# Page loads of odd samples issued by the ScalarE queue, those of even samples by the sync engine

## The reference

```
past_rows = pool[layer, page_table]            # 16 pages of 128 rows per sample, K and V, 2 heads of 128
s = q . k * HEAD_DIM ** -0.5 - slope * dist    # then a mask: the 16 best blocks of 64 rows
p = softmax(s)
o = p . v
```

## Time and profile before

| | |
|---|---|
| median of 3 runs | 3255.11 us (3253.07 to 3260.55) |
| the profiled execution's own time | 3257.21 us |
| its span, first to last instruction | 3255.5 us |
| busy: TensorE matmul, weight load | 2653.4 us (82%), 2007.5 us (62%) |
| busy: VectorE, ScalarE | 860.5 us (26%), 272.5 us (8%) |
| read from HBM, written | 669.20 MB, 17.50 MB |
| mean granted TensorE clock | 0.872 of full speed |
| the phase of the 10 turns | from 1722.9 us to 1934.5 us of the span |

### The profile page before, as it was taken

How to read it: one execution, slowest core, us unless ns; L and a number is a source line. 1 busy time by engine, 2 the same in 40 slices (tenths; PEclk the granted TensorE clock), 3 DMA queues, 4 the chain that set the end, 5 groups by cost and what they waited for, 6 DMA issues and landing times. The chain is left out here.

```text
span 3255.5 us, 46977 instructions
## 1 busy us (share of the span) xinstructions
PE 2653.4 (82%) x19541; PEld 2007.5 (62%) x19541; DVE 860.5 (26%) x2027; ACT 272.5 (8%) x598; POOL 21.1 (1%) x68
## 2 busy tenths in 40 slices
PE   5999995999982577783666459649999999999997
PEld 4767673777751576672644337546777676677764
DVE  0121212000038455415344320222111211211124
ACT  0010101000010000000112110100010010001001
POOL 0000000000000000000000000000000000000000
PEclk9999996999985688766557779859999999999998
DMA  6888854242210000001374763229999999999991
GB/s 238 318 321 316 321 193 162 103 155 103 103 39 13 15 2 2 2 1 29 109 230 105 182 186 123 84 76 405 409 392 402 396 398 392 403 394 392 399 398 44
DMA packets 180772, 679.98 MB, mean 209 GB/s; under 512 B 38188, under 2 KB 39038, under 8 KB 141918
## 3 DMA queue, kind: packets, MB, share of 16 engines
q1 hardware_dynamic: 177780, 673.92, 55.3%
q10 hardware_dynamic: 2884, 4.50, 0.4%
HBM read 669.20 MB, written 17.50 MB: 211 GB/s over the span
## 5 line engine op out<-in xcount | busy, mean ns | idle before, releaser
L571 PE MATMUL bank<-sb_hT,sb_w_in 128*128 128x296 f32 x1408 | 353.6, 415 | 3.9 <-PEq L462 3.9
L571 PEld LDWEIGHTS bank<-sb_hT,sb_w_in 128*128 128x128 f32 x1408 | 269.0, 191 | 88.5 <-issue 5.9
L2418 PE MATMUL bank<-sb_gate_w,sb_x_picked 128*64 128x256 f32 x2048 | 322.1, 379 | 0.7 <-DMA sb_up_w<-in_w_up_dram 0.7
L2418 PE MATMUL bank<-sb_up_w,sb_x_picked 128*64 128x256 f32 x2048 | 322.1, 379 | 0.0
L2443 PE MATMUL bank<-sb_down_w,sb_hiddenT 128*64 128x512 f32 x1024 | 226.8, 594 | 9.0 <-ACT sb_x_picked L2478 9.0
L397 PE MATMUL bank<-sb_cmp_xT,sb_cmp_w 128*128 128x254 f32 x1024 | 223.4, 379 | 6.7 <-ACT sb_cmp_xT L213 5.8
L397 PEld LDWEIGHTS bank<-sb_cmp_xT,sb_cmp_w 128*128 128x128 f32 x1024 | 193.2, 190 | 39.0 <-ACT sb_cmp_xT L213 8.4
L2418 PEld LDWEIGHTS bank<-sb_gate_w,sb_x_picked 128*64 128x64 f32 x2048 | 175.1, 137 | 59.9 <-issue 17.1
L2402 PE MATMUL bank<-sb_select,sb_h2rows 128*128 128x128 f32 x1632 | 188.9, 278 | 18.6 <-DVE sb_give L2512 18.6
L2418 PEld LDWEIGHTS bank<-sb_up_w,sb_x_picked 128*64 128x64 f32 x2048 | 175.3, 137 | 45.7
L2402 PEld LDWEIGHTS bank<-sb_select,sb_h2rows 128*128 128x128 f32 x1632 | 185.6, 194 | 24.9 <-DVE sb_give L2512 18.7
(11 more groups left out here) (535 smaller groups left out, 2823.9 us busy)
## 6 DMA issues: line engine op xcount, KB each, us to landing
sb_gate_w<-in_w_gate_dram SPq DMA_DIRECT2D x64, 2048.0 KB, 10.5
sb_up_w<-in_w_up_dram SPq DMA_DIRECT2D x64, 2048.0 KB, 15.0
sb_down_w<-in_w_down_dram SPq DMA_DIRECT2D x64, 2048.0 KB, 9.3
sb_w_ada<-in_w_ada_dram SPq DMA_DIRECT2D x48, 2048.0 KB, 10.9
sb_w_in<-in_w_in_dram SPq DMA_DIRECT2D x11, 4096.0 KB, 13.3
sb_cmp_raw<-in_cache_cmp_kv_dram SPq DMA_DIRECT2D x128, 256.0 KB, 7.6
sb_sample_kv<-in_cache_slc_kv_dram SPq DMA_DIRECT2D x128, 256.0 KB, 5.4
sb_w_out<-in_w_out_dram SPq DMA_DIRECT2D x4, 4096.0 KB, 13.9
```

The source lines that it names most:

```text
L571: ins = pe.matmul(k.bank[m][:, 0:NX], w[r][:, t, m * P:(m + 1) * P], k.hT[:, t, :], start=(t == 0), stop=(t == KT - 1))
L2418: ins = pe.matmul(bank[b][64 * half:64 * half + 64, col:col + 256], x[:, t, b * 64:b * 64 + 64], w[i][:, t % CK, half * 256:half * 256 + 256],
```

## The change

ScalarE issues the page units with odd m, that is those of odd samples, from unit 11 on, and the sync engine keeps the page units with even m and all windows. ScalarE does so at the end of a turn, behind `exp(n)` (in turn 3 behind `pre_exp` as well), for those of the units 4(n - 1) + 11 to 4n + 10 that are odd and no windows, after a wait for `s_av` >= n, which is the value that the sync engine waits for at these units. `load_pages` itself is the same, and so are the buffers, the semaphores that the loads raise and the units loaded ahead.

```diff
@@ the sync engine's block of phase_attend_samples
                 for m in range(N_UNITS, 4 * N_TURN):
                     if m == 12:
                         sp.wait_ge(s_pre, SCORED)
                         load_kc(k, sp, 1)
                     if m == 20:
                         sp.wait_ge(s_pav, 1)
                         load_vc(k, sp, 1)
+                    if m // 4 % (N_CH + 1) and m % 2:
+                        continue
                     sp.wait_ge(s_av, (m - N_UNITS) // 4 + 1)
                     (load_pages if m // 4 % (N_CH + 1) else load_window)(k, A, sp, m)
@@ the ScalarE block, in the loop over the turns n
                     exp(n)
                     if n == 3:
                         pre_exp(1)
+
+                    for m in range(max(N_UNITS, 4 * (n - 1) + N_UNITS), min(4 * n + N_UNITS, 4 * N_TURN)):
+                        if n and m // 4 % (N_CH + 1) and m % 2:
+                            act.wait_ge(s_av, n)
+                            load_pages(k, A, act, m)
```

## The result

The changed kernel takes **3290.56 us** in the median of 4 runs (3283.85 to 3296.36), against 3254.6 us (3253.07 to 3260.55) for the kernel before: ratio 1.0106, 95% interval 1.0082 to 1.0131. It is slower by 36 us where 26 were forecast. The median stands 0.56 us above the upper end of the range, which is less than the runs differ among themselves. The profiled execution has a span of 3291.4 us and took 3293.18.

What follows compares the result with a forecast made beforehand. TensorE's waits before turns 2 to 9 for each release's opening page unit were taken as the bound; sharing the DMA engines adds 26.6 us to 3257.21, 3283.8, less 2.1 for the median: 3281 us forecast, range 3253 to 3290.

Steps and rivals of the forecast that it cites:

- What bounds the phase: Before turns 2 to 9 TensorE waits for the unit opening each release; eight waits, 64.9 us together, on the path.
- A page's rate is set by its transfer, not its issue: Page loads: 1.17 us of DMA-engine transfer at 225 GB/s, slower than the 1.07 us issue.
- the rival: No change: two queues near 400 GB/s, opening unit lands as before, bound by issue and ScalarE's hold; 3256 us, chance 0.15.
- ScalarE's issue price of 1.07 us: Each of 52 loads added to ScalarE costs the sync engine's 1.07 us; bounds 0.32 and 1.97 us.
- the hold of 8.6 us: Issuing two units holds ScalarE 8.6 us before the next turn's key copies; hidden, at worst +11 us.
- The shared page time: Opening unit's pages interleave with the sync engine's: 3.16 + 7.5 x 1.17 = 11.9 us, against 7.84 at turn 2.
- the rule of slots: Opening unit lands 3.16 us plus a number of page times after the values; 7 to 8 when shared, 7.5 taken.
- Turn 4: Wait for unit 19, ScalarE's, beside three windows: 12.6 us against 7.84, +4.8; +7.4 if whole windows pass between pages.
- the lateness: At turn 4 ScalarE issues unit 19 some 2.2 us later than the sync engine did, behind its exponentials.
- Turns 5 and 6: Turn 5, window 23 beside ScalarE's unit 25: +3.0 us; turn 6, ScalarE 0.6 us late: 12.4 against 9.84, +2.6.
- 16 pages in a period of now 23 us, so the queues drain each time: Each turn's 16 pages take 18.7 us of transfer within a 23 us period, leaving no backlog for the next release.
- The rivals: No change, 3256 us, chance 0.15; faster, shared page time under 0.69 us (380 GB/s), 3247 us, chance 0.08.

Runs made afterwards that it cites:

- e10: Changed kernel plus a sync-engine wait: it starts its own units only when the pages of the turn ScalarE's opening unit completes have landed; 3255.55 us, ratio 1.0000.
- e5: Kernel before, all loads on the sync engine, each page spread over 128 partitions (2 KB each) instead of 32; 3243.48 us, ratio 0.9971.
- e6: Changed kernel with each page spread over 128 partitions instead of 32; 3265.2 us, ratio 1.0026 against the kernel before.
- e3: Changed kernel, but ScalarE issues only the opening page units, the sync engine the rest; 3286.91 us, ratio 1.0101 against the kernel before.
- e1: Kernel before, all on the sync engine, with pages of the first two units issued alternately in five releases; 3268.52 us, ratio 1.0060.
- e2: Changed kernel with parts swapped: even page units on ScalarE, odd (opening) ones on the sync engine; 3285.09 us, ratio 1.0094 against the kernel before.
- e4: Kernel before with each page unit from 11 on split: pages 0 and 1 on the sync engine, 2 and 3 on ScalarE; 3252.62 us, ratio 0.9995.

## Why the prediction was right, and where it was off

- *What bounds the phase* (the unit that opens a release is awaited at once) holds: e10 changes nothing but its company, and 31.5 of the 33.7 us of waits go; the time is that of the kernel before (ratio 1.0000, 0.9982 to 1.0017).
- *A page's rate is set by its transfer, not its issue*: shown by e5 and e6 (242 and 338 to 359 GB/s), where issuing is as before and the waits fall, by 7.8 and 23.7 us. Had the issue been the bound, the changed kernel would have stood at 3256, as the rival has it.
- *ScalarE's issue price of 1.07 us* measured 1.06, and the hold of 8.6 us is hidden, as costed: e3 halves it and gains nothing, and e10 keeps it and has no loss.
- *The shared page time* was too small. I took 225 GB/s and 7.5 slots, 11.9 us; turns 2, 7 and 8 show 13.5 to 13.7. At 210 GB/s a page is 1.25 us, and with 8 slots 3.16 + 8 x 1.25 gives 13.2. e1, in one queue, has 11.5 to 11.8 by seven slots, 11.4 by the formula at 225 GB/s and 11.6 at the 217 of its stretch: so the rule of slots is sound. The rate and the half slot are the mis-sized terms. They make 1.3 us of the 1.7 to 1.8 that turns 2 and 8 wait beyond the forecast. That turn 3, with the same company, waits only 12.3 stays open.
- *Turn 4*: I took 2.5 us for window packets between unit 19's pages and kept 5.1 as the upper bound (a rise of 7.4). It was 8.2, above even that. The windows made 7.1 of it and the lateness, taken at 2.2, at most 1.1, as e10 shows (8.9 with the late unit 19 alone); e2, with unit 19 early and ahead of the windows in one queue, waits 7.80.
- *Turns 5 and 6*: the step that failed is "16 pages in a period of now 23 us, so the queues drain each time". At turn 5 ScalarE's pages, issued from 1840.93, did not delay the window beside them (-0.3, not +3.0). But then only 15.2 us lay between the two releases (1840.19 to 1855.41), for 12 pages and a window, 17.5 us of transfers; what was left of them stood before unit 27, and turn 6 paid 6.0 us and not 2.6. The DMA engines were still 0.97 busy right behind the second release (1855.40 to 1858.00 in the stretches above), where they had stood still behind the first (share 0.00 from 1840 to 1841). The rows could have told it: before the change, too, these two releases are 15.6 us apart (1820.01 and 1835.63 in the earlier trace rows). The sum of the two turns, 5.6 forecast and 5.7 measured, hides this; that the total held there is luck.
- *The rivals* fell: with pages on 32 partitions two queues had at most 272 GB/s in a stretch (e4), far from 380, and the opening unit of the changed kernel landed after 12 us and more.

## What to carry to other kernels

Before a second queue is given part of the loads, find out which transfer the engines wait for, and whether the DMA engines are already full while it runs. If they are, a second queue gives no rate, it gives the awaited transfer a companion: order within one queue is a priority, and here two queues had none between them (288 packets to 283). Look also at how many partitions a transfer lands on; in this kernel spreading the pages gained 9 us (e5), and a second queue alone never gained clear of the noise.

## What I had not expected

Pages of two units in alternation, each pair on the same 32 partitions, move a little less than pages in order: 208 to 215 GB/s from two queues and 217 from one (e1), against 225. From two queues on different halves they move 234, and 272 early in a release. The stages ahead of the phase move its start from 1718 to 1736 us between profiled executions of kernels that are alike up to there, so that a single time says little about an effect of 5 us, and the waits inside the phase say much.
